# Expert weight slabs on one DMA queue or on two: the down projections move to ScalarE's queue

## The reference

```python
def expert_block(args):
    xr, e = args
    return (jax.nn.silu(xr @ w_gate[e]) * (xr @ w_up[e])) @ w_down[e]
# out[token] += y * gate[token]
```

## Time and profile before

| | us |
|---|---|
| median of 3 runs | 1945.16 |
| lowest, highest run | 1943.06, 1947.52 |
| profiled execution, its span | 1945.6 |
| TensorE busy, of the span | 1657.3 (85%) |
| ScalarE busy | 234.0 (12%) |
| DMA on SP's queue (q1), of 16 engines' span | 69.0% |
| DMA on ScalarE's queue (q10), of 16 engines' span | 1.2% |

### The profile page before, as it was taken

One profiled execution on the slowest core, in us unless ns is written; L12 is line 12 of the kernel. 1 busy time (PEld: TensorE's weight loads), 2 busy tenths in 40 slices (PEclk: granted clock), 3 DMA queues, 4 the chain that ended last, 5 costly groups with the idle time before them and its releaser, 6 DMA issues.

```text
span 1945.6 us, 22389 instructions
## 1 busy us (share of the span) xinstructions
PE 1657.3 (85%) x8945; PEld 1026.5 (53%) x8945; DVE 461.7 (24%) x976; ACT 234.0 (12%) x504; POOL 237.6 (12%) x498
## 2 busy tenths in 40 slices
PE   4799888888879787998888888799887899899998
PEld 3554444444436645544334333385776585488853
DVE  5311111111112313111111111157554201124321
ACT  2010000000021221100000000231122010200000
POOL 2000000000000000000000000049991000000000
PEclk9799999999999787999999999989888999899999
DMA  9399999999995223999999999962312425135310
GB/s 323 123 381 394 394 394 394 394 394 394 394 394 193 92 83 109 385 394 394 394 394 394 394 394 394 394 220 82 113 52 90 175 106 169 55 130 172 132 65 22
DMA packets 235222, 504.04 MB, mean 259 GB/s; under 512 B 16442, under 2 KB 42395, under 8 KB 235163
## 3 DMA queue, kind: packets, MB, share of 16 engines
q1 hardware_dynamic: 221623, 497.21, 69.0%
q10 hardware_dynamic: 13540, 6.04, 1.2%
HBM read 502.18 MB, written 1.05 MB: 259 GB/s over the span
## 4 chain that ended last, share of the span: by engine, by line
PE 45%; DMA 29%; POOL 8%; SPq 7%; DVE 5%; issue 3%; ACT 2%; ACTq 0%; POOLq 0%; DVEq 0%
DMA ring<-in_w_up 27%; PE PS L711 10%; PE PS L1166 8%; SPq L524 7%; PE PS L1176 4%; PE PS L1113 3%; PE PS L943 3%; DMA ring<-in_w_gate 2%; PE PS L754 2%; PE PS L656 2%; PE PS L1103 2%; PE PS L917 1%; PE PS L1094 1%; POOL arena L2215 1%; POOL XN L2214 1%
## 5 line engine op out<-in xcount | busy, mean ns | idle before, releaser
L711 PE MATMUL PS<-ring,arena 128*64 128x256 f32 x4096 | 470.5, 383 | 146.5 <-DMA ring<-in_w_up 85.2
L711 PEld LDWEIGHTS PS<-ring,arena 128*64 128x64 f32 x4096 | 295.0, 137 | 345.3 <-DMA ring<-in_w_up 107.9
L754 PE MATMUL PS<-ring,arena 128*64 128x512 f32 x1024 | 233.9, 598 | 1.1 <-ACT arena L1305 1.1
L1693 DVE TENSOR_TENSOR arena<-PS,arena 128x256 f32<-128x256 f32 x64 | 27.2, 425 | 868.3 <-ACT arena L1298 868.3
L2160 POOL COPY arena<-arena 128x512 f32 x64 | 60.5, 945 | 920.9 <-DVE arena L1693 857.8
L1166 PE MATMUL PS<-hT,ring 128*128 128x256 f32 x704 | 153.8, 382 | 1.0 <-issue 1.0
L754 PEld LDWEIGHTS PS<-ring,arena 128*64 128x64 f32 x1024 | 68.2, 136 | 157.8 <-issue 119.9
L1166 PEld LDWEIGHTS PS<-hT,ring 128*128 128x128 f32 x704 | 134.8, 192 | 19.9 <-issue 1.3
L740 PE MATMUL PS<-arena 64*128 64x512 f32 x512 | 127.2, 615 | 2.0 <-ACT arena L1314 2.0
L932 PE MATMUL PS<-hT,ring 128*128 128x256 f32 x448 | 100.1, 385 | 0.0
L1305 ACT ACTIVATE arena<-PS 128x256 f32<-128x256 f32 x64 | 24.6, 384 | 586.6 <-PE PS L727 586.6
(11 more groups left out here) (374 smaller groups left out, 1489.2 us busy)
## 6 DMA issues: line engine op xcount, KB each, us to landing
ring<-in_w_gate SPq DMA_DIRECT2D x64, 2048.0 KB, 19.3
ring<-in_w_up SPq DMA_DIRECT2D x64, 2048.0 KB, 21.9
ring<-in_w_down SPq DMA_DIRECT2D x64, 2048.0 KB, 19.3
ring<-in_f_w_up SPq DMA_DIRECT2D x22, 1024.0 KB, 7.6
ring<-in_w_in SPq DMA_DIRECT2D x9, 2048.0 KB, 20.7
ring<-in_f_w_down SPq DMA_DIRECT2D x5, 2048.0 KB, 7.8
ring<-in_x_wkv SPq DMA_DIRECT2D x4, 2048.0 KB, 8.1
ring<-in_wo SPq DMA_DIRECT2D x2, 2048.0 KB, 13.5
```

The lines of the kernel that those rows point to most:

```text
L711: mm = pe.matmul(PS[half * WINDOW:(half + 1) * WINDOW, bank, m * half_f:(m + 1) * half_f], xw[bank][:, k, :], mat[:, k, half * half_f:(hal ...
L754: mm = pe.matmul(PS[half * WINDOW:(half + 1) * WINDOW, 3, :], hidT[:, w, k * WINDOW:(k + 1) * WINDOW], mat[:, k, half * 512:(half + 1) * 5 ...
```

## The change

SP no longer requests the down slabs of experts 1 to 30: `on_scalar_queue(j)` leaves them out, in the peeled turns and in the loop. ScalarE requests them. It issues down 1 after its first `silus` and before its first step, and down of `e + 2` in `copy_y` of `e`, behind the wait for the end of `down` of `e` and ahead of the copy. The wait is the one that `copy_y` had before, and it is also the condition for the slot, which was down of `e`'s. Down 0 and down 31 stay with SP. ScalarE's loop over the experts runs one turn less, and that turn is written out, so that the last two experts issue nothing. The ring, its slots and the order in which TensorE uses the slabs are as before.

```diff
                 def peeled(i):
                     for j in range(i * RING, (i + 1) * RING):
+                        if on_scalar_queue(j):
+                            continue
                         if n0 + j >= RING:
                             sp.wait_ge(s["slabs_done"], n0 + j - RING + 1)
                         one(n0 + j, *expert_slab(j))
+                def on_scalar_queue(j):
+                    m, e = expert_slab(j)
+                    return m == 2 and 1 <= e < EXPERTS - 1
...
                     for k in range(RING):
-
+                        if on_scalar_queue(RING + k):
+                            continue
                         sp.wait_ge(s["slabs_done"], i * RING + (n0 + k - RING + 1))
...
+                    def load_down(n, e):
+                        down = a["w_down"][layer].rearrange("e (k p) d -> e p k d", p=P)
+                        act.dma_start(slab(n).rearrange("p (a k w) -> p a k w", a=1, w=D),
+                                      down[bass.ds(e, 1)].rearrange("a p k w -> p a k w")).then_inc(slab_loaded[n % RING], 16)
+
                     def copy_y(e, w, last):
                         if w == windows - 1:
                             act.wait_ge(s["slabs_done"], after_down(n0, e, last))
+                            if not isinstance(e[0], int) or linear(e, 1, 0) < EXPERTS - BODY - 1:
+                                load_down(n0 + PER_EXPERT * (e[1] + BODY) + 4, linear(e, 1, BODY))
...
-                    expert_steps(act, step)
+                    load_down(n0 + PER_EXPERT + 4, 1)
+                    turns = EXPERTS // BODY
+                    for b in range(BODY):
+                        step((0, b), False)
+                    with act.Fori(1, turns - 2) as i:
+                        for b in range(BODY):
+                            step((i, b), False)
+                    for turn in (turns - 2, turns - 1):
+                        for b in range(BODY):
+                            step((turn, b), turn == turns - 1 and b == BODY - 1)
```

## The result

The changed kernel takes 1961.64 us (median of 4 runs, 1958.93 to 1964.11) against 1944.11 us for the kernel before (4 runs). The ratio is 1.0085, with an interval of 1.0063 to 1.0108: slower by 16.5 us, 12 to 21. The forecast was slower, by 11.7 us (5 to 15 in its likeliest case), and 1956.9 us.

The account below looks back on a forecast made before the run. DMA at a constant 394 GB/s was taken to bound the mixtures. Order of landing 10.2, router loads 1.5, ScalarE's issues 0 and rate 0 gave +11.7 us, 1956.9 us; own range 1950 to 1962, 8 in 10 range 1942 to 1969.

Parts of the forecast that it names:

- likeliest case: Whole kernel: slower by 5 to 15 us with the DMA rate within 0.4%, chance 0.60.
- The order of landing: Mixture ends: down lands about one expert earlier, so up 31 lands 5.12 us later in each mixture; +10.2 us, bounds 0 to 10.8.
- The row it rested on: At 1262.74 a 256 KB load on ScalarE's queue landed in 5.8 us, while SP's slabs before and after took 20.7 us.
- The rate: Both mixtures: DMA rate unchanged at 394 GB/s, 0 us; ends +17 and -37 us; rivals higher 0.17, lower 0.09.
- The issue on ScalarE: ScalarE's 60 more issues, 0.36 us each with room in its queue, hide: cost 0, at most 1 us.
- The router loads: Start of layer 0's mixture: four small loads delay down 2, a DMA hole; +1.5 us, between 0 and 3; layer 1 0.
- Could TensorE itself be what is late ... so no: Mixture ends: TensorE needs at least 12.8 us from up 30 to up 31, landing 14.6 us apart, so no larger delay.
- The clock: Rival, up in the mixtures: idle before up may halve TensorE's clock; +20 us, 1977 us, if all of up; chance 0.04.
- The 0.50 of one MLA row: In MLA one idle piece of 2.80 us was enough for a granted TensorE clock of 0.50, 1.2 in place of 2.4 GHz.

Follow-up runs that it names:

- e2: The changed kernel, but ScalarE issues only the down slabs of experts 28, 29 and 30, SP all others: 1960.08 us, ratio 1.0071 against the kernel before.
- e1: The changed kernel, but SP again issues the down slabs of experts 28 to 31, ScalarE those of 1 to 27: 1952.66 us, ratio 1.0028.
- e3: The kernel before, one queue, but in each mixture's last turn SP requests down 30 ahead of gate 31 and up 31: 1959.54 us, ratio 1.0074.
- e8: The kernel before, but the router loads for layer 1 are issued ahead of layer 0's experts, at about 70 us: 1946.56 us, ratio 1.0002.
- e7: The changed kernel, but SP also issues down 30, ScalarE down 1 to 29: 1957.90 us, ratio 1.0059 against the kernel before.
- e5: The changed kernel, but ScalarE issues its own loads behind the request of down 2 and expert 0's copy of y: 1960.37 us, ratio 1.0065.
- e6: The changed kernel with the edits of e1 and e5 together: 1949.88 us, ratio 1.0020 against the kernel before.

## Why the prediction was right, and where it fell short

**The order of landing: right, with its size.** The 5.12 us for each mixture stand against e2's 4.9 and 5.7, and they go when the last downs return to SP (e1) and come with one queue alone (e3). The row it rested on, 256 KB in 5.8 us beside 20.7 us, foretold the landing of down (12.3 us, forecast 8 to 14; the sum had said 13). By the Trainium skill's rule on turns between queue rows ("DMA: Bandwidth & Descriptors", section "Queues, rings and completion order") the same was to be expected, and the trace agrees: gate and up went from 19.3 and 21.9 us to 24.4 us while down fell from 19.3 to 12.3.

**The rate: right.** 394 GB/s, in every variant with two queues too. The Trainium skill says (same page, section "Issuing engines are not separate DMA queues") that DMAs issued by several engines run on the same 16 DMA engines and save no more than sequencer time; these rates agree.

**The issue on ScalarE: right.** In the steady stretch it takes 0.38 us, with SP held beside it, as these rows of the two sequencers in the changed kernel show; and e8 found no cost of 4 us of holding.

```profile
332.69 7.24 SPq L524 DMA_DIRECT2D ring<-in_w_up  x1
```
```profile
335.13 0.38 ACTq L1318 DMA_DIRECT2D ring<-in_w_down  x1
```

**The router loads: too small.** I took 1.5 us in layer 0 and 0 in layer 1. By the bytes it was 2.7 and 0.4. The two issues in the changed kernel:

```profile
106.14 0.50 ACTq L1225 DMA_DIRECT2D arena<-in_router_expert_b  x1
106.68 0.61 ACTq L1318 DMA_DIRECT2D ring<-in_w_down  x1
```

The request itself came soon behind the router loads, as forecast, but the data did not: the DMA moved 53 GB/s from 108 to 110 and was back at 414 only from 111 on. I had allowed for the delay of the request and not for the time from there to the data. That down's rows stood behind what was left of the small packets on ScalarE's queue is my reading; no run separates it from the time that a request takes by itself.

**"Could TensorE itself be what is late ... so no": this step failed.** It assumed an even period, with up 31 landing 14.6 us after up 30 and some 3 us of wait gathered before every up. The downs are requested by TensorE's progress, so when two experts pass at 12.8 us their downs are requested close together and hold back the same up. ScalarE's requests in the changed kernel come in that rhythm, 12.8, 13.6 and 21.5 us apart:

```profile
308.78 0.38 ACTq L1318 DMA_DIRECT2D ring<-in_w_down  x1
321.56 0.38 ACTq L1318 DMA_DIRECT2D ring<-in_w_down  x1
335.13 0.38 ACTq L1318 DMA_DIRECT2D ring<-in_w_down  x1
356.62 0.38 ACTq L1318 DMA_DIRECT2D ring<-in_w_down  x1
```

The sum gave 10.8 us as the upper bound of this term; beyond their starts the mixtures lost 5.8 and 7.7 us, 13.5 in all. In layer 1 the cycle stood so that up 30 was the late one. Up 30 starts 474.17 us after the mixture's start, before 464.80: 9.4 us late, more than one down slab, and up took 5.49 for 3.67 us, another 1.8. TensorE then makes up 3.2 us, and some 8 remain. So of layer 1's 8.1 us I put 0.4 to the start, 5.1 to the one slab, and the remainder of 2.5 to the cycle and the clock. e7's layer 0 is the same effect at up 29. e5 makes the same requests at the end, but in its layer 1 the cycle stood otherwise: the last wait is for up 31, with the waits of before, and 5.7 us were lost beyond the start in place of 7.7.

```profile
1245.41 3.67 PE L718 MATMUL PS<-ring,arena 128*64 128x256 f32 x32 [1.09 <-DMA ring<-in_w_gate]
1250.72 3.67 PE L718 MATMUL PS<-ring,arena 128*64 128x256 f32 x32 [1.64 <-DMA ring<-in_w_up]
```

How the cycle arises is argued from the times of the requests; that its place decides is shown by these layers.

**The clock: right in kind.** The 0.50 of one MLA row behind 2.80 us of idle foretold a low clock behind the gathered waits, and that the slack would pay for it in the stretch: e1 has 0.93 there and pays for little more than its start. I gave it no price at the end, where nothing pays for it.

The sum in the forecast's own terms: order 10.2 (forecast 10.2), start 3.1 (1.5), cycle and clock at the end 2.5 (0), and 0.7 us in layer 0 that I cannot place: 16.5 us. The direction and the main term were foreseen. The time of 1961.64 us lies at the upper edge of the forecast's own range of 1950 to 1962, and part of that is luck: the loss itself was larger than its 5 to 15 us, and the kernel before came out 1.05 us faster this time.

## What to carry to other kernels

Here, with the DMA at its limit, a second queue did not add bandwidth, it changed the order: a transfer that was last in line overtook those that were needed first. Inside the stretch this was free; its price is the bytes that stand ahead of the last slab, so read the order there and not in the steady state. And a load issued ahead on another engine's queue should not stand behind small loads at a time when the DMA has nothing else in line; in e5 and e6 taking them out of its way gave back 2.5 to 2.8 us in layer 0.

## What the runs showed of the hardware

Two queues with 2 MB transfers of 4 KB and of 2 KB rows move the same 394 GB/s as one. While SP's sequencer was held by one issue for 7.24 us, ScalarE's issue took 0.38 us. The granted clock of TensorE was 0.50 behind waits of about 5 us, and some 2 us of work were lost each time (6.02 and 5.97 for 3.67 us), while in the same stretch it stayed at 1.00 in the kernel before, whose waits there were up to 1.8 us.
